# Hybrid attention and convolution block on 8 cores: interleaved token blocks, 64-row score matmuls, exponential with a bias, and branch projections between attention units

## The reference, cut to what matters

```python
D_MODEL, BATCH, SEQ, Q_BLOCK = 1024, 4, 4096, 128
ATTN_HEADS, ATTN_HEAD_DIM, CONV_WIDTH = 4, 64, 512
h = rms_norm(x, g_pre)
q, k, v, z_a, cb, cc, cx, z_c, ga, gc = jnp.split(h @ w_in, idx, axis=-1)   # 6144 columns
# two softmax maps per head (m = 0, 1), causal, ALiBi slope per head 2**(-8(i+1)/4)
s = q_m . k_m * 64**-0.5 - slope[head] * (qpos - kpos), masked where kpos > qpos
a = softmax(s[m=0]) - lam * softmax(s[m=1])
o = rms_norm(a @ v, subln_gain) * (1 - lam_init)
y_attn = (o * silu(z_a)) @ w_attn_o
u = causal_depthwise_conv(cc * cx, conv_w)                                  # width 3
y_conv = ((cb * u) * silu(z_c)) @ w_conv_o
y = sigmoid(ga + b_a) * y_attn + sigmoid(gc + b_c) * y_conv
return x + rms_norm(y @ w_out, g_post)
```

## Time and profile before

| | |
|---|---|
| runs | 934.71, 949.57, 1058.34 us; median 949.57 us |
| profiled execution | span of the slowest core (core 6) 940.9 us; cores 924.4 to 940.9 us; no separate time is given for it |
| PE | busy 851.0 us (90%), 5832 matmuls |
| ACT | busy 606.8 us (64%) |
| DVE, POOL | busy 360.2 us (38%), 95.1 us (10%) |
| HBM | 62.05 MB read, 8.39 MB written |
| stages on core 6 | opening 0 to 136.4, attention to 540.6, end of attention to 556.6, branches to 705.3, merge to 871.2, output to 941 us |

### The profile page before, as it was taken

How to read it: one execution, slowest core, us unless ns; L and a number is a source line. 1 busy time by engine, 2 the same in 40 slices (tenths; PEclk the granted TensorE clock), 3 DMA queues, 4 the chain that set the end, 5 groups by cost and what they waited for, 6 DMA issues and landing times.

```text
span 940.9 us, 18454 instructions; the slowest of 8 cores (924.4 to 940.9 us)
## 1 busy us (share of the span) xinstructions
PE 851.0 (90%) x5832; PEld 462.6 (49%) x5832; DVE 360.2 (38%) x828; ACT 606.8 (64%) x1290; POOL 95.1 (10%) x64
## 2 busy tenths in 40 slices
PE   0589989997899988999899959899999999999995
PEld 0245546663466635665466624344444444444442
DVE  1466723205333143323363043345662222222365
ACT  3387849993699839996599906466556555552343
POOL 0000010002000010000000000000002222222375
PEclk9999999998999989999999969899999999999988
DMA  8777200001000000001011006822121111100496
GB/s 232 233 200 257 85 1 2 2 2 48 1 2 3 13 36 2 2 2 49 1 33 38 2 1 129 184 90 68 68 90 46 67 56 59 46 1 0 127 344 246
DMA packets 18590, 67.43 MB, mean 72 GB/s; under 512 B 2920, under 2 KB 3176, under 8 KB 17968
## 3 DMA queue, kind: packets, MB, share of 16 engines
q1 hardware_dynamic: 18064, 62.05, 21.0%
q0 software_dynamic: 432, 4.19, 2.6%
HBM read 62.05 MB, written 8.39 MB: 75 GB/s over the span
## 4 chain that ended last, share of the span: by engine, by line
PE 83%; DVE 5%; issue 3%; ACT 3%; DMA 3%; SPq 1%; DVEq 0%; POOLq 0%; ACTq 0%
PE bank L757 24%; PE bank L679 17%; PE bank L648 13%; PE bank L390 7%; PE bank L404 6%; PE bank L926 6%; PE bank L879 3%; PE bank L885 3%; DMA arena<-w_in_r 3%; DVE arena L705 1%; PE bank L461 1%; PE bank L601 1%; DVE arena L726 1%; ACT arena L570 1%; PE bank L654 1%
## 5 line engine op out<-in xcount | busy, mean ns | idle before, releaser
L666 ACT ACTIVATE arena<-bank 128x512 bf16<-128x512 f32 (+3 forms) x640 | 300.0, 582 | 14.4 <-PE bank L648 12.6
L757 PE MATMUL bank<-arena 128*128 128x512 bf16 x1152 | 259.3, 384 | 4.1 <-ACT arena L824 3.6
L679 PE MATMUL bank<-arena 128*128 128x129 bf16 x2368 | 216.7, 220 | 10.1 <-ACT arena L666 6.2
L679 PEld LDWEIGHTS bank<-arena 128*128 128x128 bf16 x2368 | 160.9, 97 | 101.8 <-issue 22.0
L648 PE MATMUL bank<-arena 128*128 128x512 bf16 (+3 forms) x640 | 182.2, 365 | 3.9 <-DVE arena L394 3.7
L757 PEld LDWEIGHTS bank<-arena 128*128 128x128 bf16 x1152 | 113.3, 99 | 142.9 <-issue 11.3
L570 ACT ACTIVATE arena<-arena 128x128 bf16<-128x128 f32 x256 | 101.2, 400 | 31.8 <-DMA arena<-w_in_r 10.8
L390 PE MATMUL bank<-arena 128*128 128x512 bf16 x384 | 90.3, 395 | 10.7 <-DVE arena L394 10.7
L705 DVE COPY arena<-bank 128x387 f32<-128x387 f32 (+1 forms) x48 | 23.1, 513 | 193.7 <-PE bank L679 193.3
L404 PE MATMUL bank<-arena 128*128 128x512 bf16 x256 | 63.6, 396 | 6.3 <-DVE arena L476 4.0
L390 PEld LDWEIGHTS bank<-arena 128*128 128x128 bf16 x384 | 38.4, 101 | 59.9 <-issue 18.9
(11 more groups left out here) (81 smaller groups left out, 687.7 us busy)
## 6 DMA issues: line engine op xcount, KB each, us to landing
arena<-x_perm SPq DMA_DIRECT2D x48, 512.0 KB, 7.1
arena<-w_in_r SPq DMA_DIRECT2D x48, 512.0 KB, 3.4
out_own<-arena SPq DMA_DIRECT2D x16, 512.0 KB, 7.0
arena<-wo_r POOLq DMA_DIRECT2D x1, 2048.0 KB, 18.0
arena<-zeros SPq DMA_DIRECT2D x2, 512.0 KB, 7.6
arena<-wao_r POOLq DMA_DIRECT2D x1, 1024.0 KB, 14.2
arena<-wco_r POOLq DMA_DIRECT2D x1, 1024.0 KB, 21.5
arena<-gb SPq DMA_DIRECT2D x1, 512.0 KB, 6.9
```

What stands on the lines that cost most here:

```text
L666: p.op("act", (lambda e, m=m, buf=buf, c0=c0, pi=pi: e.activation(out=PT[m][pi][:, c0:512], in_=sbank(m, buf)[:, c0:512], func=AF.Exp, sca ...
L679: p.op("pe", (lambda e, m=m, qb=qb, j=j, pi=pi, st_flag=st_flag, h=h, lastu=(u == nu - 1): e.matmul(oacc(m, qb), lhsT=PT[m][pi][:, qb * 12 ...
L757: p.op("pe", (lambda e, kc=kc, bk=bk, tt=tt, wsrc=wsrc: e.matmul(banks[bk][:], lhsT=wsrc[:, kc, :], rhs=hT_tile(kc, tt), start=(kc == 0), ...
```

## The change

The change rewrites the program on the same frame.

- **Tokens.** The two cores of a sequence take every second block of 128 tokens (`x_perm`). So the other core's blocks on the diagonal run are narrowed like the own ones, both with a mask matmul.
- **Opening.** K and Q of all four heads are projected here (48 tiles of 8 matmuls; V as before). The other core's normalized tokens live only in two buffers. x has 4 slots instead of 8, and the norm's gain is multiplied into x.
- **Weights.** All weights come by DMAs on the POOL queue that read float32 and write bfloat16; the casts on ACT, DVE and POOL are gone. Later weights pass through a ring of 8 slots; `wz` (z_attn) has its own buffer.
- **Scores.** Map 0 contracts over rows 0 to 63, map 1 over rows 64 to 127, each into its own bank. The distance term is the bias of the exponential, one column of a table per key block and distance; one exponential serves both maps, and for head 0 it is cut to 128 queries, for head 1 to 256, for heads 2 and 3 to up to 512.
- **Order.** Groups of 512 queries outside, heads inside. Branch matmuls (`Filler`) are put between the score matmuls and the accumulating matmuls by constants in the code (`C_QK`, `C_AV`, `C_MM`, `hold`). They all use PSUM bank 7. What is left runs after attention (`fill.flush()`).
- **Functions.** SiLU and sigmoid become Tanh plus products; the per-head norm's root becomes a power on POOL.
- **`Prog`.** Buffers that share memory are registered by address (`place`), and writing one counts as writing all that overlap it.

The core of the diff (only added lines; what they replace is told above):

```diff
+    def place(self, name, off, nbytes):
+        lo, hi = off, off + nbytes
+        mine = []
+        for other, (a, b) in self.span.items():
+            if a < hi and lo < b:
+                mine.append(other)
+                self.alias[other].append(name)
+        self.span[name] = (lo, hi)
+        self.alias[name] = mine
...
+        for r in reads:
+            for n in (r, *self.alias.get(r, ())):
+                w = self.last_w.get(n)
+                if w is not None:
+                    deps.append(w)
+            if r[0] == "bank":
+                deps.extend(x for x in self.readers.get(r, ()) if x.eng != eng)
+        for r in writes:
+            for n in (r, *self.alias.get(r, ())):
+                w = self.last_w.get(n)
+                if w is not None:
+                    deps.append(w)
+                deps.extend(self.readers.get(n, ()))
+        latest = {}
+        seen = set()
...
+            for n in self.alias.get(r, ()):
+                if n in self.last_w or n in self.readers:
+                    self.last_w[n] = o
+                    self.readers[n] = []
...
+            p.op("pool", (lambda e, h=h: e.dma_start(out=wk[h], in_=w_chunk[4 + h].rearrange("p (a b) -> p a b", a=KC))),
+                 writes=[("wk", h)], dma=f"ldwk{h}")
+        for h in range(4):
+            p.op("pool", (lambda e, h=h: e.dma_start(out=wq[h], in_=w_chunk[h].rearrange("p (a b) -> p a b", a=KC))),
+                 writes=[("wq", h)], dma=f"ldwq{h}")
+        p.op("pool", lambda e: e.memset(V[:, :, :, 128:129], 1.0), writes=[("Vones",)])
...
+        def w_issue():
+            while w_state["issued"] < min(len(W_SRC), w_state["retired"] + NR):
+                n = w_state["issued"]
+                w_state["issued"] += 1
+                src = W_SRC[n]
+                src_ap = w_y[src[1]] if isinstance(src, tuple) else w_chunk[src]
+                sl = n % NR
+                p.op("pool", (lambda e, src_ap=src_ap, sl=sl: e.dma_start(out=ring[sl], in_=src_ap.rearrange("p (a b) -> p a b", a=KC))),
+                     writes=[("ring", sl)], dma=f"ldr{sl}")
...
+        def follow(n):
+            kd, i = blocks[n]
+            if kd == 2:
+                return
+            vproj(n)
+            if i % 4 == 3:
+                for h in range(4):
+                    kq_tile("k", kd, i // 4, h)
+                if kd == 0:
+                    for h in range(4):
+                        kq_tile("q", kd, i // 4, h)
+        PRE = 2
+        for n in range(PRE):
+            stage_a(n)
+        for n in range(NBLK):
+            stage_a(n + PRE)
+            stage_b(n)
+            if n >= 1:
+                follow(n - 1)
+            if n == 29:
+                w_state["issued"] = 0
+        follow(NBLK - 1)
+        w_issue()
+        p.op("pool", lambda e: e.dma_start(out=wz, in_=w_wide[1].rearrange("p (a b) -> p a b", a=KC)), writes=[("wz",)], dma="ldwz")
...
+        def mm8(lhs, rhs, rd, n=KC):
+            def make(kc):
+                def f():
+                    p.op("pe", (lambda e: e.matmul(bank(FB), lhsT=lhs(kc), rhs=rhs(kc), start=(kc == 0), stop=(kc == n - 1))),
+                         reads=rd, writes=[("bank", FB)])
+                return f
+            return lambda: [make(kc) for kc in range(n)]
...
+        def z_tile(i):
+            q = i % 4
+            tb = i % 2
+            def post():
+                z_done.add(i)
+                p.op("act", (lambda e: e.activation(out=tt_[tb], in_=bank(FB), func=AF.Tanh, scale=0.5)),
+                     reads=[("bank", FB)], writes=[("tt", tb)])
+                p.op("dve", (lambda e: e.scalar_tensor_tensor(out=sz[:, q, :], in0=tt_[tb], scalar=1.0, in1=bank(FB), op0=ALU.add, op1=ALU.mult)),
+                     reads=[("tt", tb), ("bank", FB)], writes=[("sz", q)])
+                szv = sz[:, q, :].rearrange("p (h e) -> p h e", h=4)
+                gv = gainb.unsqueeze(1).broadcast_to([128, 4, 128])
+                p.op("pool", (lambda e: e.tensor_tensor(out=szv, in0=szv, in1=gv, op=ALU.mult)),
+                     reads=[("sz", q), ("gain",)], writes=[("sz", q)])
+            n = 8 * (i // 4) + i % 4
+            return {"mm": mm8(lambda kc: hTo[:, kc, i * 128:(i + 1) * 128], lambda kc: wz[:, kc, :], [("hT", n), ("wz",)]), "post": post, "hold": 1.8}
...
+                def post_zc(b=b, t=t):
+                    utf = ut[b].rearrange("p b n -> p (b n)")
+                    p.op("act", (lambda e: e.activation(out=tt_[b], in_=bank(FB), func=AF.Tanh, scale=0.5)),
+                         reads=[("bank", FB)], writes=[("tt", b)])
+                    p.op("dve", (lambda e: e.scalar_tensor_tensor(out=tt_[b], in0=tt_[b], scalar=1.0, in1=bank(FB), op0=ALU.add, op1=ALU.mult)),
+                         reads=[("tt", b), ("bank", FB)], writes=[("tt", b)])
+                    p.op("pool", (lambda e: e.tensor_tensor(out=gconvT[:, c, t * 512:(t + 1) * 512], in0=tt_[b], in1=utf, op=ALU.mult)),
+                         reads=[("tt", b), ("ut", b)], writes=[("gconvT", c, t)])
+                    if t == 3:
+                        w_retire(4 * c + 3)
+                for k, post, hold in ((0, post_cc, 0.9), (1, post_cx, 0.9), (2, post_cb, 0.9), (3, post_zc, 1.8)):
+                    out.append({"mm": mm8(lambda kc, k=k: ring[sl[k]][:, kc, :], rhs, [("ring", sl[k])] + hr), "post": post, "hold": hold})
+            return out
...
+        def emit_qk(n):
+            s, h, kd, j, dl, mk, _, _ = units[n]
+            buf = n % 2
+            c0 = 128 * dl
+            kcol = (kd * 16 + j) * 128
+            for m in range(2):
+                p.op("pe", (lambda e, m=m: e.matmul(psum[:, 2 * buf + m, c0:512], lhsT=KT[h][64 * m:64 * m + 64, kcol:kcol + 128],
+                                                    rhs=QT[h][64 * m:64 * m + 64, s * 512 + c0:(s + 1) * 512], start=True, stop=(mk is None))),
+                     reads=[("KT", h, kd, j // 4), ("QT", h, s)], writes=[("bank", 2 * buf + m)])
+            if mk is not None:
+                for m in range(2):
+                    p.op("pe", (lambda e, m=m: e.matmul(psum[:, 2 * buf + m, c0:c0 + 128], lhsT=identb, rhs=mask[:, mk * 128:(mk + 1) * 128],
+                                                        start=False, stop=True)),
+                         reads=[("identb",), ("mask",)], writes=[("bank", 2 * buf + m)])
+        def emit_exp(n):
+            s, h, kd, j, dl, mk, _, _ = units[n]
+            buf = n % 2
+            sl = n % NPT
+            sh = SHARE[h]
+            for r_ in range(0, 4, sh):
+                if r_ + sh <= dl:
+                    continue
+                lo = max(r_, dl)
+                idx = j - (4 * s + r_) + 16
+                col = (h * 2 + kd) * NTAB + idx
+                p.op("act", (lambda e, lo=lo, hi=r_ + sh, col=col: e.activation(
+                    out=PT[sl][:, :, lo * 128:hi * 128], in_=psum[:, 2 * buf:2 * buf + 2, lo * 128:hi * 128], func=AF.Exp,
+                    bias=tab[:, col:col + 1], scale=0.125)),
+                     reads=[("bank", 2 * buf), ("bank", 2 * buf + 1), ("tab",)], writes=[("PT", sl, qb) for qb in range(lo, r_ + sh)])
+        def emit_av(n, started):
+            s, h, kd, j, dl, mk, _, last = units[n]
+            sl = n % NPT
+            vj = kd * 16 + j
+            order = [(m, qb) for qb in range(dl, 4) for m in range(2)] if SHARE[h] < 4 else [(m, qb) for m in range(2) for qb in range(dl, 4)]
+            for m, qb in order:
+                acc, bid = oacc(m, qb)
+                first = bid not in started
+                started.add(bid)
+                p.op("pe", (lambda e, m=m, qb=qb, acc=acc, first=first: e.matmul(
+                    acc, lhsT=PT[sl][:, m, qb * 128:(qb + 1) * 128], rhs=V[:, vj, h, :], start=first, stop=last, skip_group_check=True)),
+                     reads=[("PT", sl, qb), ("V", vj), ("Vones",)], writes=[("bank", bid)])
...
+        C_QK, C_AV, C_MM = 0.33, 0.0566, 0.214
+        pe_t = act_t = fb_t = 0.0
+        started = set()
+        g = 0
+        emit_qk(0)
+        for n in range(NU):
+            s, h, kd, j, dl, mk, first, last = units[n]
+            if first:
+                started = set()
+            emit_exp(n)
+            w_ = 4 - dl
+            calls = sum(1 for r_ in range(0, 4, SHARE[h]) if r_ + SHARE[h] > dl)
+            act_t = max(act_t, pe_t - 0.6) + calls * 0.16 + w_ * 256 / 1200.0
+            if n + 1 < NU:
+                emit_qk(n + 1)
+                pe_t += C_QK
+            while len(fill) and pe_t + C_AV * 2 * w_ < act_t + 0.15 and (fill.open or pe_t >= fb_t):
+                r_ = fill.step()
+                if r_ is None:
+                    break
+                pe_t += r_[0]
+                if r_[1]:
+                    fb_t = pe_t + r_[1]
+            pe_t = max(pe_t, act_t - 0.2) + C_AV * 2 * w_
+            emit_av(n, started)
+            if last:
+                while side:
+                    side.pop(0)()
```

(19 more changed lines are left out.)

1254 lines of the change are left out of this document (532 added, 722 removed).

## The result

The changed kernel takes **1207.69 us** (median of 4 runs, 1204.39 to 1208.52), the kernel before 943.25 beside it (4 runs). The ratio is **1.284**, 95% interval 1.275 to 1.293: slower by 28%, where 932 us was forecast and 868 to 990 given as range. The profiled core has a span of 1207.0 us.

What follows compares the result with a forecast made beforehand. Attention was taken as bound by ACT with PE close behind, other stages by PE. Opening 176, wz wait 12, attention 380, its end 9, left-over branches 119, merge 166 and output 70 sum to 932 us; range 868 to 990.

Steps and rivals of the forecast that it cites:

- Merge and output: 166 and 70 us, as before: Last two stages: PE's matmuls cover Tanh, products and sum; residual loads, stores and tail unchanged, so 166 and 70 us.
- Opening, 176 us: Opening stage: 44 us until the last Q weights, then 132 us of PE work, up from 136 us.
- PE is held there by Q weights: Opening: Q tiles behind the fourth block wait for the last Q weights, taken as 44 us, from 41 to 58.
- Attention, 380 us: Attention, bound by ACT: 315 + 36 + 11 + 10 + 8 = 380 us, down from 404; PE beside it 329 us.
- The loop of heads 2 and 3: Attention: next scores need the bank the exponential frees, making 1.05 us a unit against 0.98; 10 us more.
- Sixteen changes of group cost 0.5 us each: Attention: a small term for moving from one group to the next, 8 us in the sum.
- Left-over branches, 128 us: After attention: 9 us end of attention plus 119 us for 302 matmuls, with waits for evictions of bank 7.
- rival 3: Left-over stage runs at the lower clock: 64 us more, total 996, or 964 if it comes back midway; chance 0.11.
- Wait for wz, 12 us: Before the first accumulating matmul: PE waits for the wz load behind eight ring loads; 12 us, bounds 6 and 20.
- 1: Attention: ACT's waits are covered and the half arrays free, so 336 us there, total 888; chance 0.26.
- 2: Attention: PE becomes the bound through the pair of score matmuls, from 0.51 us a pair; at 0.71 total 1012; chance 0.09.
- 4: Attention: Tanh and Exp switch tables on ACT, total 988; chance 0.04.

Runs made afterwards that it cites:

- x1_alias: The changed kernel, but writing a buffer no longer makes it last writer of every buffer overlapping it: 1066.6 us, 1.128 of the kernel before.
- x8_both: x4_all with the moves of x6_ahead and x7_swap, K and Q weight loads held back, Q tiles behind the other core's K tiles: 912.6 and 914.3 us, 0.973 of before.
- x2_htp: The changed kernel with a separate name for each block of an hTp buffer: 1161.8 us, 1.228 of the kernel before.
- x7_swap: x4_all with VectorE's copy of block n ahead of the norm of block n+2, and wz loaded ahead of the ring: 934.1 us, 0.992 of before.
- x6_ahead: x4_all with the scores of unit n+2 issued ahead of the accumulating matmuls of unit n: 954.0 us, 1.017 of the kernel before.
- x11_nobias: x8_both with no bias in the exponentials: a single execution of 935.6 us, so no ratio.
- x9_order: x8_both with attention's query blocks in the order 3, 2, 1, 0: 910.1 to 912.3 us, 0.9615 of before; some gated tiles overwritten before they are transposed.
- x12_zfirst: x8_both with the first four z tiles through banks 4 to 7 before the first accumulating matmul: 904.0 to 910.1 us, 0.966; some gated tiles overwritten before transposing.
- x13_keep: x12_zfirst with each gate waiting until the transposes of group g-2, which read the same buffer, are issued: 914.3 us, 0.974 of before.
- x3_flush: The changed kernel with left-over branch tiles taking the eight banks in turn instead of bank 7 alone: 1147.7 us, 1.214 of the kernel before.
- x4_all: The changed kernel with the three edits of x1_alias, x2_htp and x3_flush together: 965.2 us, 1.021 of the kernel before.
- x14_orderk: x9_order with each gate waiting until the transposes of group g-2 are issued: 907.9 to 908.7 us, 0.967 of before.
- x5_full: x4_all with score matmuls contracting over all 128 rows, so the two maps are not kept apart: 960.5 us, 1.024 of the kernel before.

## Why the prediction was wrong

By its own steps, largest first; the five differences make up the whole 275 us.

1. **"Merge and output: 166 and 70 us, as before"** failed by 108 us, and was the step with the least work in it. It looked at engines and bounds of the stage, all of which still hold: x1_alias brings back 165.8 and 67.5. What it did not look at is what each write waits for by name. The same step had the rule in hand: the forecast's own 36 us for exponentials that wait for exponentials come from it (the P tiles and an opening buffer share a place). I applied it to attention alone.
2. **Opening, 176 us**: the terms of work were right (x8_both is 184, with PE full from 40 us on), the wait was missing. Of the 83 us, 50 are the shared name of hTp (x2_htp) and 19 VectorE's order (x7_swap). Of the last 15, 7 come back when the weights are held back (x8_both; 10 in the median of the cores). In place of "PE is held there by Q weights", PE waited for x: the fifth block, asked for at some 11 us, landed at 37.2 to 40.0 by core in the changed kernel, beside twelve weight loads.
3. **Attention, 380 us**: found by its mechanism, and too small. Waits through joined names: 36 forecast, 26 found; the pace is the forecast's, 0.57 us where an exponential waits for the one before and 0.36 where not, 0.46 in the mean. The loop of heads 2 and 3: 10 forecast, 10 to 13 found over all heads (x6_ahead). The bias: 0.085 forecast, 0.09 found (x11_nobias). The 1024-column exponential passes in 1.00 us, near the 0.98 forecast, but comes every 1.08, since PE takes 1.10 for a unit with a branch matmul. PE's sum was mis-sized: 329 us forecast, 359 busy in x8_both, and the pair, 0.42 us where 0.35 was taken, makes 22 of these 30. What was missing is that the sum took ACT as bound and everything else as cover. ACT holds 352 and PE 359 of 419.8 us in x8_both; each waits for the other in program order, and taking 46 us from ACT alone moves 5. "Sixteen changes of group cost 0.5 us each" was the weakest term: in the first query block a group's exponentials are shorter than VectorE's chain (9 to 10 us), which no move of the z tiles or of the block's place removed (x9_order, x12_zfirst, x13_keep). How much of the 69 us that chain has is not measured by itself: it was never taken away alone, and this stays open.
4. **Left-over branches, 128 us**: 142. The gaps of 0.94 us came as worked out and the gates' are 1.76 where 1.91 was taken; the tile behind the convolution's sum (L726) mostly waits 1.60, not 0.94; and the first four tiles and one later ran at half the clock, with part of a sixth: 5 x 1.7 + 1.2 = 10 us. This is a small part of rival 3. The forecast could have seen the cure: x3_flush has this stage at 76.
5. **Wait for wz, 12 us**: 6.6 (and 7 to 11 in x4_all, where the opening is shorter), inside its bounds.

**The rivals.** 1: ACT's waits were not covered, it fell. 2: the pair costs 0.42 us against 0.35 forecast and 0.51 for its threshold; PE did not become the bound alone. Of the rule cited for it, that a change of tiling mode drains the engine ("TensorEngine Tiling (Array Packing)" of the Trainium skill, Tiling Modes), the rows show a price of 0.10 us on the way in (0.153 less 0.057, from the last accumulating matmul to the pair) and 0.10 on the way out (0.32 less 0.22, the stream of 512 columns, if the two run side by side), where the forecast had allowed 0.17 each. 3: only 10 us of it. 4: fell, no table load beside Tanh, as the Trainium skill's "ScalarE: Activation LUTs" (Table sets) has it. All four rivals were about engines. The case that came, that dependencies get coarser, had no chance of its own; the range excluded it.

## What to carry to other kernels

When a change touches the allocation or the names by which dependencies are recorded, a stage with unchanged instructions is not unchanged: list for each stage what its first and its hundredth write wait for, and price the longest of them. Give every tile that is written by itself a name of its own, and let overlapping places order writes without becoming each other's writers. In a stage where two engines are each over 80% busy in turn, moving work off one pays little; here it paid more, 10 to 13 us, to have a second unit of work ready. Compare short groups with the fixed chain behind them before reordering anything: two moves of the work around that chain (x13_keep, x14_orderk) gained under 1% here.

## What the runs showed of the hardware

- A pair of half-array matmuls of 512 columns on different rows and banks overlaps: 0.32 us to the next instruction, against 0.43 for two whole ones. But going from whole to half array took 0.10 us, and back 0.10, so the pair saved nothing beside whole-array neighbours (x5_full: 960.5 against 965.2 us).
- The granted clock was lower where PE waited in turn: behind waits of 2.56 and 4.06 us in the opening eight matmuls took 3.3 and 3.4 us and not 1.73, at a clock of 0.51 and 0.50; behind one of 8.03 us in the left-over stage four tiles in a row took 3.57 us, with waits of 0.7 to 1.8 us between them, and the fifth 1.89 behind a wait of 0.94. In the output stage of the changed kernel the mean was 0.75, in that of x8_both 0.93. So the wait of 4.06 us came with 1.6 us more in the matmuls behind it.
- A bias from memory added 0.09 us to an exponential, of 256, 512 or 1024 columns alike (x11_nobias).
